# Keys, values and queries of a two-layer mixer as pairs of tiles with seven block products, and the rotation with channels on partitions

## What is computed

```python
h = rms_norm(x, norm_g)
proj = h @ w_in
(q, k, v, z_a, p_in, z_b, u, v_sgu, z_c, glu_a, glu_b, z_d,
 merge) = jnp.split(proj, SPLIT_POINTS, axis=-1)
q = apply_rope(rms_norm(q.reshape(B, S, N_Q_HEADS, HEAD_DIM), q_norm_g), cos, sin)
k = apply_rope(rms_norm(k.reshape(B, S, N_KV_HEADS, HEAD_DIM), k_norm_g), cos, sin)
v = v.reshape(B, S, N_KV_HEADS, HEAD_DIM)
o_a = window_attention(q, k, v, attn_sinks)
o_c = spatial_gating(u, v_sgu, sgu_ln_g, sgu_ln_b, sgu_w, sgu_b)
```

## Time and profile before

| | us |
|---|---|
| median of 3 runs | 2060.28 (2059.11 to 2060.38) |
| span of the profiled execution | 2057.5 |
| TensorE busy | 2049.7 |
| VectorE busy | 1366.5 |
| GpSimd busy | 1259.9 |
| ScalarE busy | 882.2 |

### The profile page before, as it was taken

How to read it: one execution, slowest core, us unless ns; L and a number is a source line. 1 busy time by engine, 2 the same in 40 slices (tenths; PEclk the granted TensorE clock), 3 DMA queues, 4 the chain that set the end, 5 groups by cost and what they waited for, 6 DMA issues and landing times.

```text
span 2057.5 us, 27183 instructions
## 1 busy us (share of the span) xinstructions
PE 2049.7 (100%) x9680; PEld 1700.8 (83%) x9680; DVE 1366.5 (66%) x1629; ACT 882.2 (43%) x1659; POOL 1259.9 (61%) x950
## 2 busy tenths in 40 slices
PE   9999999999999999999999999999999999999999
PEld 8898877888888888888888888878888888888887
DVE  5896544788878645338769964438888786453484
ACT  6624664343233334324655256543432343443242
POOL 3367444776769667554723664447766697675545
PEclk9999999999999999999999999999999999999999
DMA  7103232313431343413421122233134213434132
GB/s 277 52 32 103 88 103 98 95 60 74 94 75 52 83 82 75 141 52 117 144 89 47 42 98 97 87 104 97 52 83 96 65 52 82 92 72 143 42 133 103
DMA packets 108006, 183.63 MB, mean 89 GB/s; under 512 B 13664, under 2 KB 23136, under 8 KB 107872
## 3 DMA queue, kind: packets, MB, share of 16 engines
q1 hardware_dynamic: 88656, 151.13, 22.9%
q0 software_dynamic: 9216, 16.78, 5.9%
q10 hardware_dynamic: 10000, 13.98, 1.9%
HBM read 139.90 MB, written 41.95 MB: 88 GB/s over the span
## 4 chain that ended last, share of the span: by engine, by line
PE 96%; DVE 2%; ACT 1%; DVEq 0%; issue 0%; DMA 0%; SPq 0%; ACTq 0%
PE acc L725 81%; PE aux L794 6%; PE acc L794 4%; DVE flo L1531 1%; PE aux L869 1%; PE aux L888 1%; PE aux L879 1%; PE aux L903 1%; PE aux L831 0%; PE acc L831 0%; PE aux L845 0%; ACT fhi L995 0%; DVEq L1795 0%; DVE csum_lo L1531 0%; DMA allp<-cols 0%
## 5 line engine op out<-in xcount | busy, mean ns | idle before, releaser
L656 POOL TENSOR_TENSOR wlo<-raw,whi 128x512 fp32r<-128x512 f32 x392 | 550.6, 1406 | 491.8 <-ACT whi L995 490.8
L725 PE MATMUL acc<-fhi,whi 128*128 128x512 f32 x2024 | 793.3, 392 | 2.0 <-DVE v L1528 2.0
L725 PE MATMUL acc<-fhi,wlo 128*128 128x512 f32 x2024 | 788.9, 390 | 0.0
L725 PE MATMUL acc<-flo,whi 128*128 128x512 f32 x2024 | 788.6, 390 | 0.0
L725 PEld LDWEIGHTS acc<-fhi,whi 128*128 128x128 f32 x2024 | 380.1, 188 | 83.5 <-issue 4.3
L725 PEld LDWEIGHTS acc<-fhi,wlo 128*128 128x128 f32 x2024 | 380.1, 188 | 79.3
L725 PEld LDWEIGHTS acc<-flo,whi 128*128 128x128 f32 x2024 | 380.3, 188 | 77.2
L656 POOL TENSOR_TENSOR wlo<-wsum,whi 128x512 fp32r<-128x512 f32 x210 | 299.1, 1424 | 210.3 <-ACT whi L995 209.6
L995 ACT ACTIVATE whi<-raw 128x512 fp32r<-128x512 f32 x392 | 245.2, 626 | 385.0 <-PE acc L725 331.1
L1535 DVE SCALAR_TENSOR_TENSOR aux<-conv,allp,aux 128x1024 f32<-128x1024 f32 x232 | 299.0, 1289 | 20.4 <-issue 0.9
L995 ACT ACTIVATE whi<-wsum 128x512 fp32r<-128x512 f32 x210 | 131.9, 628 | 203.8 <-PE acc L725 159.9
(11 more groups left out here) (210 smaller groups left out, 2486.3 us busy)
## 6 DMA issues: line engine op xcount, KB each, us to landing
raw<-wstream SPq DMA_DIRECT2D x392, 256.0 KB, 2.7
md<-prev POOLq DMA_DIRECT2D x64, 256.0 KB, 4.2
x<-x SPq DMA_DIRECT2D x32, 256.0 KB, 5.0
md<-prev SPq DMA_DIRECT2D x32, 256.0 KB, 3.6
out<-x ACTq DMA_DIRECT2D x32, 256.0 KB, 2.1
mx<-md SPq DMA_DIRECT2D x24, 256.0 KB, 5.1
xrow<-x_rows SPq DMA_DIRECT2D x8, 512.0 KB, 6.8
qd<-qst ACTq DMA_DIRECT2D x16, 256.0 KB, 2.2
```

The costliest lines, as they stand in the source:

```text
L656: nc.gpsimd.tensor_tensor(wlo[:, f % SLOTS, :], src, whi[:, f % SLOTS, :].bitcast(F32), ALU.subtract).then_inc(lo_made, 1)
L725: mm = nc.tensor.matmul(dst, w, m[:, kt0 + k, cols], start=first and k == 0 and n == 0, stop=last and k == UK - 1 and n == 2, skip_group_c ...
```

## The change

The stages KV (one pair: k's tile and v's tile) and Q (two pairs) become pairs with seven products and stand behind VS: KV, Q, U, ZC. A pair of Q holds the low 32 channels of four heads in one tile and the high 32 in the other, so that the rotation needs no crossing of partitions. The activations' seven operands are therefore needed from the first product of KV on, and they are formed under VS and KV. DVE scales `x11` and `x22` in one step, while for `x12` and `x21` ScalarE multiplies by the gain (`gain_scaled`) and Pool by the norms (`h_scale` there, four tiles of 512 columns each); Pool also makes F7 (`form_7`). F6 has a buffer of its own, `f6`, which F4 then takes over. The last unit of VS does tiles 0 to 3 first, and ScalarE takes VS out of PSUM between the roundings of the forms.

For the heads, ScalarE squares both halves (`square_a`, `square_b`), DVE adds them, the sum is split in high and low, and TensorE multiplies it by a matrix with ones in blocks (`head_sums`), which leaves the head's sum on every partition. ScalarE makes the inverse root by a logarithm and an exponential (`inverse_root`). DVE rotates k (`rotate_k`) and q (`rotate_q`, per pair two times `turn` and `join`, 16 operations of 512 columns). k's other half comes by four DMAs (`swap_k`); q is stored by eight DMAs a pair (`store_q`). TensorE transposes only v (`turn_v`). The reference computation is the same.

```diff
-PLAIN = (("VS", 8), ("Q", 8), ("KV", 4))
-STAGES = (("U", 2), ("ZC", 2), ("MC", 4), ("GLU", 4), ("ZA", 2), ("MA", 4), ("P", 2), ("ZB", 2), ("MB", 4),
+PLAIN = (("VS", 8),)
+STAGES = (("KV", 1), ("Q", 2), ("U", 2), ("ZC", 2), ("MC", 4), ("GLU", 4), ("ZA", 2), ("MA", 4), ("P", 2), ("ZB", 2), ("MB", 4),
...
+                load_pair(L, "KV", 0)
+                load_pair(L, "Q", 0)
+                load_rope(L)
+                swap_k(L)
...
+            def h_scale(L, half, ks):
+
+                for k in ks:
+                    t = 1 - half
+                    block_ = x_block(UK * half + k, t)
+                    pool.wait_ge(g_scaled, 8 * L + UK * half + k + 1)
+                    nc.gpsimd.tensor_tensor(block_, block_, spreads[:, t * HALF:(t + 1) * HALF], ALU.mult
+                                            ).then_inc(h_pooled, 1)
+
+            def form_7(L, n):
+                pool.wait_ge(form_made, form_n(L, MADE, "F5", n))
+                pool.wait_ge(h_scaled, 8 * L + 4 + 2 * (n + 1))
+                at = slice(2 * n, 2 * n + 2)
+                nc.gpsimd.tensor_tensor(x12[:, at, :], x22[:, at, :], x12[:, at, :], ALU.subtract).then_inc(f7_made, 1)
...
+                    if st == "KV":
+                        pe.wait_ge(form_ready, form_n(L, RESTS, NEEDS[q], 0))
+
+                        def half(q=q):
+                            pe.wait_ge(form_ready, form_n(L, RESTS, NEEDS[q], 1))
+                        pe.wait_ge(vs_taken, 8 * L + (2 if bank in "ab" else 4))
...
-                token_major(L, "VS", 8)
-                token_major(L, "Q", 8)
-                token_major(L, "KV", 4, {0: lambda L=L: row_sums(L), 2: lambda L=L: sgu_mix(L, (0, 1))})
-                pe.wait_ge(sgu_taken, 4 * L + 2)
-                pair(L, "U", 0, {"p7": lambda L=L: sgu_mix(L, (2, 3))})
-                pair(L, "U", 1, {"p2": lambda L=L: (pe.wait_ge(ident_loaded, 16), turn_q(L, 0)),
-                                  "p4": lambda L=L: turn_q(L, 1)})
-                pair(L, "ZC", 0, {"p6": lambda L=L: turn_q(L, 2), "p2": lambda L=L: turn_q(L, 3)})
-                pair(L, "ZC", 1, {"p1": lambda L=L: turn_k(L)})
+                token_major(L)
+                pair(L, "KV", 0)
+                pair(L, "Q", 0, {"p1": lambda L=L: row_sums(L), "p4": lambda L=L: head_sums(L, 0)})
+                pair(L, "Q", 1, {"p6": lambda L=L: sgu_mix(L, (0, 1)), "p7": lambda L=L: turn_v(L)})
+                pair(L, "U", 0, {"p1": lambda L=L: head_sums(L, 1)})
+                pair(L, "U", 1, {"p6": lambda L=L: sgu_mix(L, (2, 3)), "p4": lambda L=L: head_sums(L, 2)})
+                for i in range(2):
+                    pair(L, "ZC", i)
...
+                    "p1": lambda: (square_a(L, 0), square_b(L, 0)), "p6": sgu_scales,
+                    "p5": lambda: square_high(L, 0), "p2": lambda: normal_vs(L, 0, range(TT)),
+                    "p3": lambda: inverse_root(L, 0)})
...
+                dve.wait_ge(mix_high, L + 1)
+                sub(srow[:, 1, :], sgt[:].rearrange("p g i -> p (g i)"),
+                    srow[:, 0, :].bitcast(F32)).then_inc(mix_low, 1)
+                dve.wait_ge(spread_loaded, 16 * (L + 1))
+                for k in range(UK):
+                    h_scale(L, k, 0)
+                for k in range(UK, KT):
+                    h_scale(L, k, 1)
+                form_rest(L, "B11")
+                form(L, "F5")
+                dve.drain()
+                form(L, "F6")
+                form_rest(L, "F6")
+                form_rest(L, "F5")
+                form_rest(L, "F7")
+                form_rest(L, "B21")
+                sum_x(L, "KV", 0)
+                sum_v(L, "KV", 0)
+                form_rest(L, "B22")
+                form(L, "F4")
+                sum_22(L, "KV", 0, vraw[:, HALF:SEQ])
+                form_rest(L, "F4")
...
+                gate_pair(L, "ZC", 0, branch_c, 0, 0, {"x": turns[0], "v": turns[1], "22": turns[2], "12": turns[3]})
```

More of the change, by code:

```diff
@@ L544, in _ @@
                     load_row(t)
+            load_rows(sp, 0)
             sp.wait_ge(norms_stored, 16)
@@ L702, in _ @@
                         low(L, w21, st, i, "p7")
+                        if st == "KV" and L == 0:
+                            h_scale(L, 1, range(UK))
                         w12 = loaded(L, st, i, "w12")
@@ L717, in _, with three @@
         def _(pe):
-            def three(dst, hi, lo, slot, kt0, first, last, cols=slice(0, HALF), resumed=False):
+            def three(dst, hi, lo, slot, kt0, first, last, cols=slice(0, HALF), resumed=False, half=None):
                 for k in range(UK):
+                    if half and k == UK // 2:
+                        half()
                     wh = whi[:, slot, k * P:(k + 1) * P]
@@ L797, in token_major @@
-                        if n_tile == 3 and k == n - 1 and name != "KV":
+                        slot = (L * FORMS + FORM["VS", kx]) % SLOTS
+                        s = X_SLOT[kx // UK, tile // 4]
+                        at = slice(tile % 4 * P, (tile % 4 + 1) * P)
+                        for m, (h, w) in enumerate(((fhi, whi), (flo, whi), (fhi, wlo))):
+                            mm = nc.tensor.matmul(tile_bank(tile), h[s][:, kx % UK, at], w[:, slot, :],
+                                                  start=kx == 0 and m == 0, stop=kx == KT - 1 and m == 2)
@@ L849, in turn_k, with head_sums @@
-            def turn_k(L):
-                pe.wait_ge(turn_taken, 9 * L + 6)
-                pe.wait_ge(roped, 6 * L + 6)
+            def head_sums(L, n):
+                pe.wait_ge(qk_low, 3 * L + n + 1)
+                if n:
+                    pe.wait_ge(sgu_taken, 4 * L + n + 1)
+                else:
+                    pe.wait_ge(vs_taken, 8 * L + 8)
+                for t in range(2):
+                    at = slice(t * HALF, (t + 1) * HALF)
+                    nc.tensor.matmul(aux[:, n % 2, at], bones_r[:], sqh[:, at], start=True, stop=False)
+                    mm = nc.tensor.matmul(aux[:, n % 2, at], bones_r[:], tmp_r[n][:, at], start=False, stop=True)
+                mm.then_inc(qk_summed, 1)
@@ new lines, in square_b, with square_high @@
+            def square_b(L, n):
+                st, i = QK_AT[n]
+                if n:
+                    act.wait_ge(taken["d"], bank_n(L, "d", (st, i), 2))
+                    act.wait_ge(roped, 3 * L + n)
+                else:
+                    act.wait_ge(swapped, 16 * 4 * (L + 1))
+                    act.wait_ge(row_summed, L + 1)
+                nc.scalar.activation(sqs[:], QK_B[n][:], ACT.Square).then_inc(qk_squared, 1)
+            def square_high(L, n):
+                act.wait_ge(qk_added, 3 * L + n + 1)
+                copy(sqh[:], tmp[n][:]).then_inc(qk_high, 1)
@@ L1771, in merge_block @@
                 bank = BANK_OF[q]
-                gate_buf = {"B11": s1[:], "B12": v1[:], "B22": y1[:], "B21": xs[:, i % 2, :]}[q]
+                gate_buf = {"B11": s1[:], "B12": v1[:], "B22": y1[:], "B21": xs_of(st, i)}[q]
                 dst = gate_buf
```

699 lines of the change are left out of this document (328 added, 371 removed).

## The result

The changed kernel takes 2138.2 us (median of 4 runs, 2134.6 to 2139.4) against 2060.3 (2059.1 to 2060.4) for the kernel before, run beside it: 1.0376 times as long, 95% interval 1.0362 to 1.0391. Its profiled execution has a span of 2137.2 us, 79.7 more than before. The forecast was 2125 with a range of 2085 to 2150. So the direction was right and the size 13 us short.

What follows compares the result with a forecast made beforehand. TensorE, busy for the whole span, was taken as the bound. From 2060.3 us, -20.7 saved, +49.8 KV stops, +2 x 1.3 for sgu_mix and +2 x 16.4 for rotations gave +64.5, 2125 us; range 2085 to 2150.

Steps and rivals of the forecast that it cites:

- TensorE's saving: From the end of VS to the first scores, fewer matmuls and transposes save 10.4 us a layer, 20.7 in both.
- KV, 26.6 + 23.2 us: TensorE's stops from the end of VS through KV, layers 0 and 1, as DVE and Pool take turns: 49.8 us.
- the first stops: Between VS and KV's first product, TensorE waits for F6 and ScalarE's take of VS: 9.6 and 10.5 us.
- p4's: Stop ahead of KV's product p4, which waits for F4 to be formed, rounded and subtracted: 6.3 and 6.4 us.
- p7's 1.9 and 1.7: Stops ahead of KV's product p7 in layers 0 and 1; in layer 1 for its low part.
- the ends of 1.3 and 4.0: Bounds in us for each of Pool's two F7 operations in KV; 2.3 was taken.
- The third rival, the clock: TensorE's clock falls behind every stop over 5 us, and slow products add 11 us; 12%.
- DVE doesn't get the port whenever ready: Denies the rival that DVE always gets the port and Pool is pushed back: KV stops 9 us, 2053 us, 7%.
- The rotations don't hide: Denies the rival that q's rotations in U and ZC cost nothing while KV's stops remain: 2092 us, 13%.
- Q's stop ahead of sgu_mix: In Q1, sgu_mix waits 1.3 us a layer for ScalarE's inverse root.
- The swapped key: In Q, k's other half arrives by DMA about 6.5 us behind KV, costing nothing while a 3 us cover stands.
- The step that failed: Storing and loading q around ZC and MC costs nothing, or 1 to 2 us; MC's attention stays as before.

Runs made afterwards that it cites:

- run 12: Changed kernel with DVE's and Pool's scalings of h and F7 cut to 8 columns, no q rotation, srow and MC0's weight loads moved; 2069.0 us.
- Run 4: Changed kernel with 45 idle zero-weight matmuls on TensorE behind the last VS product of each layer; 2137.5 us.
- run 7: Changed kernel with idle zero-weight matmuls on TensorE in three stops of each layer, in U0 and ZC1; 2138.0 us.
- runs 5 and 8: Changed kernel with DVE's srow moved behind F7's rest, 2134.8 us; the same with all sixteen scalings of h on DVE, 2135.2 us.
- run 3: Changed kernel with the rotation and scaling of q left out, one 8-column copy signalling instead; 2099.7 us.
- run 6: Changed kernel with SP issuing MC0's first four weight blocks ahead of the load of q; 2130.5 us.
- Run 10: Changed kernel with Pool forming F7 over 8 columns only, all waits kept; 2130.9 us.
- Run 9: Changed kernel with the two sgu_mix groups in Q1 one product later; 2138.8 us.

## Why the prediction was right, and where it was not

**TensorE's saving**, 10.4 us a layer: right. The stretch of run 12 has the pace on which it rests, to 0.2 us in 99.

**KV, 26.6 + 23.2 us:** right in the sum (26.4 + 24.0), not in its parts. (In layer 0 its own parts make 17.2 to 17.8 inside KV, where it added up 17.) The chains were right: bank a free at 61.76 where 60.6 was forecast, the first stops 10.4 and 10.3 where 9.6 and 10.5 were forecast, p2's 6.45 for 6.4, p4's in layer 1 5.0 for 6.4. But p7's 1.9 and 1.7, p3's in layer 0 and half of it in layer 1, and more than half of p4's in layer 0 didn't come. F7 took Pool 3.35 us an operation between DVE's turns, within the ends of 1.3 and 4.0 and above the 2.3 taken, so it was no shorter chain that saved them. The lowered clock made TensorE come later: idle is 19.9 and 18.3, and 6.5 and 5.7 us of slow products stand in the place of the rest. Run 4 shows it: with p1 at full pace p7 stops 1.4 and 1.6 us. The two make up for each other because KV ends with DVE's queue, which the forecast had worked out, whatever TensorE does meanwhile; that the sums agree to 0.8 us is still luck, as the same KV differs by 1 to 2.7 us from run to run.

**The third rival, the clock:** its premise came true and its price was wrong. The clock falls behind every stop over 5 us, as it said (the granted clock over 51.45 to 98.40 is 0.75, the idle time included), and behind shorter ones. By the Trainium skill (TensorE: Matmul & The Clock Gate, Part 1) an idle TensorE comes back at the lower level; the trace agrees, with matmuls 0.43 us apart behind the stop of 10.41. But its 11 us don't add. Run 4 takes slow products away and the time stays, since the next product waits for DVE or Pool in either case; run 7 does it in U and ZC, where it is less clean. Only a slow product with no later wait behind it costs: the last one of KV (4.7 us and not 2.7 in layer 1), `sgu_mix`, and the one behind the stop in MC0. That sum came close to 2138 for the wrong reason. The missing 13 us lie at stops that the rival didn't count: 9.6 in MC0, of which 3.7 are slow matmuls, and 5.2 at `sgu_mix`, of which 3.2 are. So the clock is about half of what the forecast lacked, in places where neither it nor the rival had it.

**The other rivals** fell. DVE doesn't get the port whenever ready (runs 5 and 8). The rotations don't hide: run 3 gives them 16.0 and 14.9 us in U and ZC, where 16.4 was the sum. The parts were again shifted: stops of 5.7 in U and 4.9 in ZC (layer 0), the rest slow products. The 1.2 us for an operation of 512 columns was sound: start to start the sixteen in U0 took 18.6 us, 1.16 each, and those in ZC0 17.3, 1.08 each.

**Q's stop ahead of sgu_mix:** forecast 1.3, measured 2.2 and 2.35, and 5.1 and 5.2 us to the next product instead of 3.6 for `sgu_mix` at the lowered clock. That is 2.5 and 2.7 us short. The swapped key was whole 7.0 us behind KV (6.5 forecast); the chain of waits runs through it (6.78 us for its last DMA, from 1160.85).

**The step that failed** is the one on `store_q`: "In MC the attention is as before, the q loads are issued a tile pair ahead." I followed the q that is stored and loaded, and the engine that waits for it, and priced at nothing or at 1 to 2 us. What I did not follow is what SP has behind the store: it stands at the last rotation of q1, then issues eight stores and q's load, and only then MC0's weights. In layer 0 Pool can form their first sum at 239.7, the last rotation ended at 226.4. They hold ScalarE, thus DVE, thus the softmax. It cost 9.6 us for both layers, 7.7 of which run 6 brought back by moving four loads ahead.

**What is still open.** Run 10 gave two thirds of what the turns of DVE and Pool were to give; where the last third went was not followed. That F4's stop would shrink if Pool's weight operations stood elsewhere follows from the rows of run 12, but no run moved them. Why the stops of layer 0 differ from run to run by 1 to 2.5 us is not known. Run 9 was not a clean test of what the inverse root alone costs.
